# First norm from token-major sums and column halves of the conditioning; conditioning pieces closed one iteration later

## The chip, the cores and the metric

One NeuronCore of a Trainium2 chip runs the whole kernel. The metric is the device time of one execution in microseconds (us). Three runs of the kernel before gave 1294.48, 1294.83 and 1295.87 us, a median of 1294.83 us.

## The reference

One decoder layer for 512 tokens of width 1024, all in f32. A vector c of 1024 numbers is turned into nine vectors (shift, scale and gate for three sublayers), which steer the rest:

```python
mod = (silu(c) @ w_ada + b_ada).reshape(b_, 3, 3, d)           # w_ada: 1024 x 9216
h = modulate(rms_norm(x, norm_gains[0]), mod[:, 0, 0], mod[:, 0, 1])
x = x + 0.5 * mod[:, 0, 2] * swiglu(h, ffn1_w_in, ffn1_w_down) # 1024 -> 2 x 2816 -> 1024
h = modulate(rms_norm(x, norm_gains[1]), mod[:, 1, 0], mod[:, 1, 1])
...                                                            # projection, two gated recurrences, merge
x = x + mod[:, 1, 2] * (merged @ w_out)
h = modulate(rms_norm(x, norm_gains[2]), mod[:, 2, 0], mod[:, 2, 1])
x = x + 0.5 * mod[:, 2, 2] * swiglu(h, ffn2_w_in, ffn2_w_down)
return rms_norm(x, final_norm)
```

## The kernel before, in words

**Layout.** Activations lie channel-major: `X` is eight blocks of 128 channels by 512 tokens. Weights come in units of 1 MB (8 k-blocks by 256 columns) into `RAW`, two slots in turn. Each f32 value is split into a high and a low part: ScalarE writes the high part (`WH`, L873, `split_hi`), VectorE the rest (`WL`, L1200, `split_lo`), and TensorE takes three products per k-block and half of the columns (`three`, L478 to L480: WH by HH, WH by HL, WL by HH), 48 matmuls of 512 columns a unit. `HH` and `HL` are the same split of the normalised activation. Semaphores written by hand set the whole order: each engine has one list of instructions, and `unit_hi`, `unit_lo`, `unit_done`, `h_lo` count units and blocks.

**The conditioning.** The product silu(c) @ w_ada is made on VectorE: a piece is 512 columns of `w_ada`, and for each of the eight k-blocks `ada_term` (L1297, L1300) adds weight times one value per partition to `ACC`. A piece is closed on TensorE by eight one-column matmuls against ones, two for each 128 columns (`ada_reduce`, L608), and VectorE adds the bias into `MOD` (`add_ada_bias`, L1332). There are 18 pieces. The first four (shift and scale of the first sublayer) go through `ADA0`, 8 MB in eight transfers of two k-blocks; the other 14 through the two `ADAW` buffers, four transfers each (`load_ada`, L328), each of the last two waiting until VectorE is done with the buffer.

**The start.** x arrives token-major in `XST`. TensorE transposes it into channel blocks (L592), ScalarE copies each out of PSUM into `X` and squares it into `SG` (L882), GpSimd adds the squares into `S` (L423), TensorE sums over the partitions with a matmul against ones (L581), ScalarE makes the inverse root (`RMS`). Meanwhile VectorE works off the four pieces of `ADA0`, TensorE closes them (L599), VectorE makes scale and shift vectors (`vectors0`), splits the first unit, and then `normalise` and `norm_blocks` make block after block of `HH` and `HL`; the first unit's k-loop waits for each block.

**The loop of the first feed-forward part.** Eleven iterations of two units each (gate, up). In iteration i TensorE closes a piece of the conditioning before k-block 5 of the up unit; VectorE splits the next gate unit, adds that piece's bias (and so waits for the close), works off the next piece, multiplies gate by up (L1346), splits the next up unit. SyncE loads two units and a piece per iteration. After the loop the down projection closes two more pieces, and `first_units` of the mixing part the last one.

**The two later norms.** The last unit of a stage is done by token halves (`last_unit`), and `half_sum` (L551, L553, L556) sums squares of a half: three products, of `S` (blocks 0 to 5), of `SG` block 6 and of `SG` block 7, each as two matmul instructions.

## Time and profile before

| | |
|---|---|
| three runs, median | 1294.83 us |
| the profiled execution | 1293.82 us, of which its span is 1292.1 us |
| TensorE matmul busy | 1235.5 us (96%), 6099 matmuls |
| VectorE busy | 599.9 us (46%) |
| ScalarE busy | 415.4 us (32%) |
| GpSimd busy | 85.2 us (7%) |
| DMA | 143.40 MB, mean 111 GB/s |
| the three products of a k-block, activation side (L478 to L480) | 1064 times each, 383 to 392 ns a piece |

The busy share of TensorE is near the whole span, so what matters is where it does not run, or runs at the lower of its clock levels; VectorE and ScalarE are idle for half and more of the span. The span differs from the execution's time by 1.7 us, which lie before and after the first and last instruction.

### The profile page before, as it was taken

How to read it: one execution, taken by the hardware profiler on the slowest of the kernel's cores; microseconds unless marked ns; L12 is line 12 of the kernel's file. 1: busy time of each engine (PE TensorE's matmuls, PEld its weight loads, DVE VectorE, ACT ScalarE, POOL GpSimd, SP SyncE). 2: the span in 40 equal slices, each digit the busy share in tenths (PEclk: the TensorE clock that was granted, in tenths of full speed). 3: DMA queues.
4: the chain of work that ended last, by engine and by line, in shares of the span. 5: the costliest groups of instructions: out<-in, count | busy, mean ns of one | idle time of the engine just before them, and what ended most of it. 6: DMA issues, size and time to landing. Idle time of an engine off the chain costs nothing.

```text
span 1292.1 us, 15169 instructions
## 1 busy us (share of the span) xinstructions
PE 1235.5 (96%) x6099; PEld 1021.0 (79%) x6099; DVE 599.9 (46%) x714; ACT 415.4 (32%) x442; POOL 85.2 (7%) x121
## 2 busy tenths in 40 slices
PE   4699999999999999989999999999999999999996
PEld 3578888888889997867887788888988888888885
DVE  6855556456343667456645333335523233232221
ACT  4522322222222365343434322223422222222222
POOL 5100000000000032022310000000000000000000
PEclk9999999999999999988999999999999999999998
DMA  9276555555252422111221222243123332222311
GB/s 379 66 241 193 172 171 178 195 184 165 90 184 93 131 65 66 35 39 60 66 66 33 66 83 85 93 130 98 48 83 97 97 97 97 97 89 67 114 57 65
DMA packets 119789, 143.40 MB, mean 111 GB/s; under 512 B 3892, under 2 KB 102336, under 8 KB 119744
## 3 DMA queue, kind: packets, MB, share of 16 engines
q1 hardware_dynamic: 119560, 142.69, 33.6%
q8 instruction: 33, 0.54, 0.2%
q14 instruction: 12, 0.10, 0.0%
q10 hardware_dynamic: 184, 0.07, 0.0%
HBM read 140.65 MB, written 2.10 MB: 110 GB/s over the span
## 4 chain that ended last, share of the span: by engine, by line
issue 48%; PE 39%; DVE 6%; ACT 3%; DMA 2%; POOL 1%; SPq 0%; ACTq 0%; POOLq 0%; DVEq 0%
PE PS L478 10%; PE PS L480 10%; PE PS L479 10%; PE PS L682 3%; DVE ACC L1300 2%; PE PS L608 1%; ACT WH L873 1%; PE PS L521 1%; DMA RAW<-in_w_in_mix_dram 1%; PE PS L522 1%; PE PS L523 1%; DMA RAW<-in_ffn_w_in_dram 1%; DVE W L1440 1%; PE PS L722 1%; DVE WL L1200 0%
## 5 line engine op out<-in xcount | busy, mean ns | idle before, releaser
L478 PE MATMUL PS<-HH,WH 128*128 128x512 f32 (+1 forms) x1064 | 416.9, 392 | 7.4 <-DVE HL L1222 4.0
L479 PE MATMUL PS<-HL,WH 128*128 128x512 f32 (+1 forms) x1064 | 408.1, 384 | 0.0
L480 PE MATMUL PS<-HH,WL 128*128 128x512 f32 (+1 forms) x1064 | 408.0, 383 | 0.0
L1200 DVE TENSOR_TENSOR WL<-RAW,WH 128x2048 fp32r<-128x2048 f32 (+1 forms) x97 | 216.9, 2236 | 345.1 <-ACT WH L873 345.1
L873 ACT ACTIVATE WH<-RAW 128x2048 fp32r<-128x2048 f32 (+1 forms) x97 | 180.8, 1864 | 407.8 <-PE PS L480 370.6
L478 PEld LDWEIGHTS PS<-HH,WH 128*128 128x128 f32 x1064 | 201.2, 189 | 53.1 <-issue 6.8
L480 PEld LDWEIGHTS PS<-HH,WL 128*128 128x128 f32 x1064 | 201.1, 189 | 43.2
L479 PEld LDWEIGHTS PS<-HL,WH 128*128 128x128 f32 x1064 | 201.4, 189 | 41.3 <-issue 1.1
L478 PE MATMUL PS<-UH,WH 128*128 128x512 f32 (+1 forms) x372 | 140.2, 377 | 0.0
L479 PE MATMUL PS<-UL,WH 128*128 128x512 f32 (+1 forms) x372 | 139.8, 376 | 0.0
L480 PE MATMUL PS<-UH,WL 128*128 128x512 f32 (+1 forms) x372 | 139.6, 375 | 0.0
L1300 DVE SCALAR_TENSOR_TENSOR ACC<-ADAW,COND,ACC 128x512 f32<-128x512 f32 x98 | 73.7, 752 | 58.9 <-DMA ADAW<-in_w_ada_dram 56.2
L480 PEld LDWEIGHTS PS<-UH,WL 128*128 128x128 f32 x372 | 70.1, 188 | 13.7
L478 PEld LDWEIGHTS PS<-UH,WH 128*128 128x128 f32 x372 | 70.0, 188 | 13.6
L479 PEld LDWEIGHTS PS<-UL,WH 128*128 128x128 f32 x372 | 70.1, 188 | 13.5
L682 PEld LDWEIGHTS PS<-QP,KP 128*128 128x128 f32 (+1 forms) x384 | 50.8, 209 | 15.7 <-DVE KP L1455 10.5
L682 PE MATMUL PS<-QP,KP 128*128 128x64 f32 (+1 forms) x384 | 52.5, 294 | 8.8 <-DVE KP L1455 8.8
L980 ACT ACTIVATE SG<-PS 128x1024 f32<-128x1024 f32 x22 | 22.6, 1027 | 118.9 <-PE PS L480 116.7
L1346 DVE TENSOR_TENSOR SG<-SG,PS 128x1024 f32<-128x1024 f32 x22 | 26.8, 1218 | 60.2 <-PE PS L480 60.2
L1471 DVE COPY_PREDICATED SC<-MASK,PS 128x256 f32<-128x256 int8 x48 | 25.6, 533 | 42.3 <-PE PS L682 41.3
L882 ACT ACTIVATE SG<-X 128x512 f32<-128x512 f32 x28 | 17.7, 631 | 85.2 <-DVE X L1361 82.3
L984 ACT ACTIVATE UH<-SG 128x1024 f32 x22 | 23.2, 1053 | 63.7 <-DVE SG L1346 63.7
(225 smaller groups left out, 1187.6 us busy)
## 6 DMA issues: line engine op xcount, KB each, us to landing
RAW<-in_ffn_w_in_dram SPq DMA_DIRECT2D x44, 1024.0 KB, 5.2
ADAW<-in_w_ada_dram SPq DMA_DIRECT2D x56, 512.0 KB, 5.6
RAW<-in_w_in_mix_dram SPq DMA_DIRECT2D x22, 1024.0 KB, 5.2
RAW<-in_ffn_w_down_dram SPq DMA_DIRECT2D x16, 1024.0 KB, 5.2
ADA<-in_w_ada_dram SPq DMA_DIRECT2D x8, 1024.0 KB, 14.0
RAW<-in_ffn_w_down_dram SPq DMA_DIRECT2D x7, 768.0 KB, 4.8
RAW<-in_w_out_dram SPq DMA_DIRECT2D x3, 1024.0 KB, 5.1
XST<-in_x_dram SPq DMA_DIRECT2D x4, 512.0 KB, 5.1
```

Of the source, the lines that this page charges most:

```text
L478: mm(ps, whi, ahi, start=start, stop=False)
L479: mm(ps, whi, alo, start=False, stop=False)
L480: return mm(ps, wlo, ahi, start=False, stop=stop)
L682: ins = mm(PS[:, bank, 256 * j + 64 * t:256 * j + 64 * t + 64], KP[r, l, t * P:(t + 1) * P], QP[r, l, 64 * t:64 * t + 64], start=True, sto ...
L873: A(WH[slot(n)][:, 0:size], RAW[slot(n)][:, 0:size], ACT.Copy).then_inc(unit_hi, 1)
L882: A(SG[:, b % 2, :], ap, ACT.Square).then_inc(sq_ready, 1)
L980: A(SG[:, :, :], PS[:, 0:2, :], ACT.Silu).then_inc(silu_done, 1)
L984: A(UH[:, ds(2 * i, 2), :], SG[:, :, :], ACT.Copy).then_inc(u_hi, 1)
L1200: V.tensor_tensor(WL[s][:, 0:size], RAW[s][:, 0:size], WH[s][:, 0:size].bitcast(F32), ALU.subtract)\
L1300: V.scalar_tensor_tensor(acc_tile, w, COND[:, k:k + 1], acc_tile, ALU.mult, ALU.add).then_inc(ada_acc, 1)
L1346: V.tensor_tensor(SG[:, :, :], SG[:, :, :], PS[:, 2:4, :], ALU.mult).then_inc(umul_done, 1)
L1471: ins = V.copy_predicated(near, m, ps).then_inc(near_done, 1)
```

## The change

It rebuilds the start. The first four pieces of the conditioning are cut by columns into two halves: each half holds, for shift and for scale, the columns of four channel blocks, and is worked off with terms of 1024 columns instead of 512; k-block 1 of the first half goes to TensorE. `ADA0` comes in 16 transfers of one k-block, rows of 2 KB instead of 4 KB, and the first units' RAW comes in k-halves behind each half of `ADA0`. Sums of squares are made from token-major x on ScalarE (`accum_out`), one number per token, and the normalised blocks come from TensorE as x times a diagonal matrix of inverse roots (`normalised`), parked in `TN0`. The transposes that give `X` are spread between. The first two units run as k-blocks 0 to 3 of both, then 4 to 7 of both (`first_pair`). GpSimd no longer adds squares.

Each later piece is loaded and worked off one iteration later and closed in the gate unit of the iteration after; the last four are closed in the down projection (three) and in the output projection (one). At the two later norms the next unit's split is cut in two halves, the squares of block 6 are added to `S` on VectorE, and the sums take three products instead of six. The small inputs all go on ScalarE's queue; the two sigmoids of the lower bound move behind the loop.

```diff
-        ADA0 = place("ADA0", [P, 2, DB, 2 * AW], 0)
+        ADA0 = place("ADA0", [P, 2, DB, 2, AW], 0)
         XST = place("XST", [P, TT, D], 65536)
-        ACC0 = place("ACC0", [P, 4, AW], HO + 2 * H_BYTES - 4 * AW * 4)
+        ACC0 = [place("ACC0a", [P, 2 * AW], NT), place("ACC0b", [P, 2 * AW], 2 * FB * T * 4)]
+        TN0 = place("TN0", [P, DB, T], HO + H_BYTES)
+        DIAG = place("DIAG", [P, TT, P], 104448)
...
+        PE_TERMS = ((1,), ())
+        TN0_BANK = (4, 5, 7, 3, 4, 5, 7, 4)
+        TN0_AFTER = {4: 1, 5: 2, 6: 3, 7: 5}
...
+            def load_ada0(half):
+                for k in range(DB):
+                    sp.dma_start(ADA0[:, half, k, :, :], ada_parts[:, k, 0:2, AW * half:AW * (half + 1)])\
+                        .then_inc(ada0_in[DB * half + k], 16)
...
-            load(0, 0, raw(0), cols(w1, 0))
-            load(1, 1, raw(1), cols(w1, FF))
-            load_ada(4 * DB, slice(4 * AW, 5 * AW))
-
+            KH = DB // 2
+            load_ada0(0)
+            for n, col in ((0, 0), (1, FF)):
+                sp.dma_start(raw(n)[:, 0:KH, :], cols(w1, col, 0, KH)).then_inc(low_in[n], 16)
+            load_ada0(1)
+            for n, col in ((0, 0), (1, FF)):
+                sp.dma_start(raw(n)[:, KH:DB, :], cols(w1, col, KH, KH)).then_inc(raw_in[n], 16)
...
-                load_ada(5 * DB + DB * i, ds(AW * i + 5 * AW, AW))
+                load_ada(4 * DB + DB * i, ds(AW * i + 4 * AW, AW))
...
-                if j in (1, 5):
-                    piece = NP + 4 + (1, 5).index(j)
+                if j in (2, 5, 8):
+                    piece = NP + 3 + j // 3
...
+                if pair == 1:
                     piece = NP + 6
+                    sp.wait_ge(y_lo, 2 * HEADS)
                     load_ada(DB * piece, slice(piece * AW, (piece + 1) * AW))
...
-            nc.gpsimd.memset(S[:, :], 0.0).then_inc(sacc, 1)
-            for b in range(DB):
-                pool.wait_ge(sq_ready, b + 1)
-                pool.wait_ge(sacc, b + 1)
-                nc.gpsimd.tensor_tensor(S[:, :], S[:, :], SG[:, b % 2, :], ALU.add).then_inc(sacc, 1)
...
-                            if (th, m, k) == (1, 0, 4):
-                                at_mid()
+                            if (th, m, k) == sum_at:
+                                half_sum(e + 1, 0)
...
                 ps = PS[:, 7 - th, half_t(th)]
-                if blocks67 != 1:
-                    pe.wait_ge(sacc, 9 + 7 * g)
-                    if th and g == 1:
-                        pe.wait_ge(mod_ready, NP + 6)
+                if th == 0:
+                    pe.wait_ge(sacc, SACC_LAST[g] + 8)
                     mm(ps, ONES[:, :], S[:, half_t(th)], start=True, stop=False)
-                    pe.wait_ge(sq_ready, 8 + 10 * (g - 1) + 7 + 2 * th)
-                    mm(ps, ONES[:, :], SG[:, 0, half_t(th)], start=False, stop=False)
-                if blocks67 != 0:
-                    pe.wait_ge(sq_ready, 8 + 10 * (g - 1) + 8 + 2 * th)
+                    pe.wait_ge(sq_ready, 8 + 10 * (g - 1) + 8)
                     mm(ps, ONES[:, :], SG[:, 1, half_t(th)], start=False, stop=True).then_inc(ssq_done, 1)
-
-            def first_units(n0, banks, g, between=None):
+                else:
+                    pe.wait_ge(sacc, SACC_LAST[g] + 10)
+                    pe.wait_ge(mod_ready, NP + 5 + g)
+                    mm(ps, ONES[:, :], S[:, half_t(th)], start=True, stop=True).then_inc(ssq_done, 1)
...
+            def normalised(b):
+                if b in TN0_AFTER:
+                    pe.wait_ge(tn_copied, TN0_AFTER[b])
+                for t in range(TT):
+                    ins = mm(PS[:, TN0_BANK[b], t * P:(t + 1) * P], XST[:, t, b * P:(b + 1) * P], DIAG[:, t, :],
+                             start=True, stop=True)
+                ins.then_inc(tn_done, 1)
...
+            def ada0_reduce(half):
+                pe.wait_ge(ada_acc, 16 * half + 16)
+                for s, m, col in ada0_columns(half):
+                    whole = not PE_TERMS[half]
+                    ins = mm(PS[:, 6, col:col + 1], ACC0[half][:, AW * s + m * P:AW * s + (m + 1) * P],
+                             ONES[:, 0:1], start=whole, stop=whole or (s, m) == (1, 3))
+                ins.then_inc(ada_red, 2)
+            for b in (0, 1, 2):
+                transpose_x(b)
+            pe.wait_ge(cond_ready, 1)
+            for k in PE_TERMS[0]:
+                pe.wait_ge(ada0_in[k], 16)
+                for j, (s, m, col) in enumerate(ada0_columns(0)):
+                    mm(PS[:, 6, col:col + 1], ADA0[:, 0, k, s, m * P:(m + 1) * P], COND[:, k:k + 1],
+                       start=k == PE_TERMS[0][0] and j == 0, stop=False)
+            pe.wait_ge(small_ready, 1)
+            pe.wait_ge(dg_ready, TT)
+            for b in range(4):
+                normalised(b)
+            pe.wait_ge(xready, 3)
+            transpose_x(3)
+            ada0_reduce(0)
+            for b in (4, 5):
+                normalised(b)
...
+            def first_pair():
+                for n in range(2):
+                    pe.wait_ge(low_lo, n + 1)
+                    whi, wlo = weights(n)
+                    for k in range(DB // 2):
+                        if n == 0 and k == 3:
+                            normalised(6)
+                        if n == 1 and k == 1:
+                            normalised(7)
+                        if n == 1 and k == 2:
+                            for b in (4, 5, 6):
+                                pe.wait_ge(tn_copied, b + 2)
+                                transpose_x(b)
+                        if n == 1 and k == 3:
+                            pe.wait_ge(mod_ready, 2)
+                            ada0_reduce(1)
+                        pe.wait_ge(h_lo, k + 1)
+                        for m in range(2):
+                            w = slice(m * P, (m + 1) * P)
+                            three(PS[:, 2 * n + m, :], whi[:, k, w], wlo[:, k, w], HH[:, k, :], HL[:, k, :], k == 0, False)
...
-                             before=ada_reduce_at(5, 5 * DB + DB * i, 4 + i) if with_ada and half == 1 else None)
+                             before=ada_reduce_at(5, 4 * DB + DB * i, 3 + i) if with_ada and half == 0 else None)
...
+                ins = A(TN0[:, 2 * t:2 * t + 2, :], XST[:, t, :], ACT.Square, accum_out=SS[:, t:t + 1])
+            ins.then_inc(ss_done, 1)
+            act.wait_ge(consts, 7)
+            act.wait_ge(ss_done, 1)
+            A(R4[:, :], SS[:, :], ACT.Ln, bias=EPST[:, 0:1], scale=1.0 / D).then_inc(first_ln, 1)
+            act.wait_ge(first_ln, 1)
+            A(R4[:, :], R4[:, :], ACT.Exp, scale=-0.5).then_inc(first_r, 1)
+            act.wait_ge(first_r, 1)
+            for t in range(TT):
+                A(DIAG[:, t, :], IDENT[:, :], ACT.Copy, scale=R4[:, t:t + 1]).then_inc(dg_ready, 1)
...
+            low_half(0)
+            act.wait_ge(av_half, 1)
+            first_block(0)
+            first_block(1)
+            low_half(1)
+            first_block(2)
+            first_block(3)
+            for b in range(4, DB):
+                park(b)
+            for b in range(4, 7):
+                copy_x(b, b + 1)
+            for n in range(2):
+                act.wait_ge(raw_in[n], 16)
+                A(WH[n][:, half_unit:UNIT], RAW[n][:, half_unit:UNIT], ACT.Copy).then_inc(unit_hi, 1)
+            act.wait_ge(av_ready, 1)
+            for b in range(4, DB):
+                first_block(b)
+            copy_x(7, 8)
...
+            def next_hi(n, part):
+                if part == 0:
+                    act.wait_ge(raw_in[slot(n)], raw_value(n))
+                    act.wait_ge(unit_done, n - 1)
+                half = UNIT // 2
+                cut = slice(part * half, (part + 1) * half)
+                A(WH[slot(n)][:, cut], RAW[slot(n)][:, cut], ACT.Copy).then_inc(unit_hi if part else next_half, 1)
+            def last_blocks(g, x0, sacc0, n):
+                if g == 1:
+                    next_hi(n, 0)
+                    next_hi(n, 1)
...
-                half_block(g, 0, 2)
-                half_block(g, 0, 3)
+                for b in range(2, 6):
+                    half_block(g, 0, b)
                 half_rms(g, 1)
-                for b in range(4, DB):
...
+            for k in range(DB):
+                if k not in PE_TERMS[0]:
+                    ada0_term(0, k)
+            low_split(0)
+            vectors0(0)
+            dve.wait_ge(tn_copied, 1)
+            first_lo(0)
+            first_lo(1)
+            low_split(1)
+            first_lo(2)
+            ada0_term(1, 0)
+            first_lo(3)
+            for k in range(1, DB):
+                ada0_term(1, k)
+            high_split(0)
+            vectors0(1)
+            first_lo(4)
+            first_lo(5)
+            high_split(1)
+            first_lo(6)
+            first_lo(7)
...
```

(`low_split` and `high_split` are `split_lo` on half a unit, `park` copies a normalised block from PSUM to `TN0`, `first_block` makes `HFULL` and `HH` of a block, `first_lo` its `HL`, `ada0_term` is a term of 1024 columns, `vectors0(half)` the bias and scale of one half.)

TensorE's list from its first instruction (PST: small inputs; XST: x; ACC: sums of conditioning terms; HH, WH: activation and weight, high parts). Before:

```order
L586 MATMUL PS<-IDENT,PST 128x124
L592 MATMUL PS<-IDENT,XST 128x128 x32
L581 MATMUL PS<-S,ONES 128x512
L599 MATMUL PS<-ONES,ACC_72 128x1 x16
...
L478 MATMUL PS<-HH,WH 128x512
```

And in the change:

```order
L598 MATMUL PS<-IDENT,PST 128x124
L603 MATMUL PS<-IDENT,XST 128x128 x12
L633 MATMUL PS<-COND,ADA_70 128x1 x8
L611 MATMUL PS<-DIAG,XST 128x128 x16
L603 MATMUL PS<-IDENT,XST 128x128 x4
L623 MATMUL PS<-ONES,ACC0a 128x1 x8
L611 MATMUL PS<-DIAG,XST 128x128 x8
L494 MATMUL PS<-HH,WH 128x512
```

Sixteen of the 32 transposes, the sum of squares and half of the closing matmuls no longer stand ahead of the first product; eight one-column products of the conditioning and 24 products with the diagonal now do.

VectorE's list from the end of the start into the loop (ADAW: the later pieces; SG: gate times up). Before, where the first of the later pieces stood ahead of the loop:

```order
L1222 TENSOR_TENSOR HL<-HFULL,HH 128x512 x2
L1297 TENSOR_SCALAR ACC<-ADAW_65,COND 128x512
L1300 SCALAR_TENSOR_TENSOR ACC<-ADAW_65,COND,ACC 128x512
...
L1200 TENSOR_TENSOR WL<-RAW,WH 128x2048
...
L1332 TENSOR_TENSOR MOD<-PS,PT 128x4
```

And in the change, where this is iteration 0, written out ahead of the loop:

```order
L1496 TENSOR_TENSOR HL<-HFULL,HH 128x512 x2
L1344 TENSOR_TENSOR WL<-RAW,WH 128x2048
L1461 TENSOR_SCALAR ACC<-ADAW_65,COND 128x512
L1464 SCALAR_TENSOR_TENSOR ACC<-ADAW_65,COND,ACC 128x512
...
L1556 TENSOR_TENSOR SG<-SG,PS 128x1024
L1344 TENSOR_TENSOR WL<-RAW,WH 128x2048
```

The piece has moved behind the split of the next gate unit.

## Rows read from the trace of the kernel before

**Rows 1.** The page: TensorE's share of the span

```profile
PE 1235.5 (96%) x6099; PEld 1021.0 (79%) x6099; DVE 599.9 (46%) x714; ACT 415.4 (32%) x442; POOL 85.2 (7%) x121
```

**Rows 2.** Timeline of TensorE, 8 to 48 us: start, length, work, [idle before <- releaser]

```profile
9.22 3.62 PE L592 MATMUL PS<-IDENT,XST 128*128 128x128 f32 x16
...
27.48 2.08 PE L581 MATMUL PS<-S,ONES 128*128 128x512 f32 x2 [9.35 <-POOL S L423]
29.35 3.57 PE L599 MATMUL PS<-ONES,ACC 128*128 128x1 f32 x16
39.52 3.58 PE L599 MATMUL PS<-ONES,ACC 128*128 128x1 f32 x16 [6.59 <-DVE ACC L1300]
47.11 0.77 PE L478 MATMUL PS<-HH,WH 128*128 128x512 f32 x1 [4.01 <-DVE HL L1222]
```

**Rows 3.** The chain that ended last, 9 to 48 us: start, length, work

```profile
13.83 4.17 DVE ACC L1300 x4
...
34.65 2.12 DVE ACC L1300 x4
...
46.27 0.69 DVE HL L1222
```

**Rows 4.** DMA in 40 slices of 1 us, 0 to 40 us

```profile
GB/s 0 36 202 381 401 419 408 428 415 430 414 418 430 414 430 414 422 422 418 430 414 430 414 422 422 414 434 379 388 379 347 351 349 199 0 0 0 0 0 33
```

**Rows 5.** Timeline of ScalarE, 9 to 44 us

```profile
10.01 1.28 ACT L962 ACT_TABLE_LOAD   x1
...
12.92 0.60 ACT L967 ACTIVATE X<-PS 128x512 f32<-128x512 f32 x1
...
43.61 0.81 ACT L944 ACTIVATE HH<-TN,MOD,AV 128x512 fp32r<-128x512 f32 x1 [7.29 <-DVE AV L1282]
```

**Rows 6.** The page: groups of instructions, xcount | busy, mean ns | idle before

```profile
L1200 DVE TENSOR_TENSOR WL<-RAW,WH 128x2048 fp32r<-128x2048 f32 (+1 forms) x97 | 216.9, 2236 | 345.1 <-ACT WH L873 345.1
L873 ACT ACTIVATE WH<-RAW 128x2048 fp32r<-128x2048 f32 (+1 forms) x97 | 180.8, 1864 | 407.8 <-PE PS L480 370.6
...
L984 ACT ACTIVATE UH<-SG 128x1024 f32 x22 | 23.2, 1053 | 63.7 <-DVE SG L1346 63.7
```

**Rows 7.** Timeline of TensorE, 51 to 53 us

```profile
51.51 0.63 PE L479 MATMUL PS<-HL,WH 128*128 128x512 f32 x1
...
51.94 0.44 PE L480 MATMUL PS<-HH,WL 128*128 128x512 f32 x1
...
52.44 0.40 PE L479 MATMUL PS<-HL,WH 128*128 128x512 f32 x1
```

**Rows 8.** The chain that ended last, 60 to 125 us

```profile
95.11 0.79 PE PS L608 x8
...
118.31 0.79 PE PS L608 x8
```

**Rows 9.** Timeline of VectorE in one iteration of the loop, 96 to 110 us

```profile
96.17 0.16 DVE L1332 TENSOR_TENSOR MOD<-PS,PT 128x4 f32 x1 [2.03 <-PE PS L608]
96.32 0.49 DVE L1297 TENSOR_SCALAR ACC<-ADAW,COND 128x512 f32<-128x512 f32 x1
...
105.91 1.22 DVE L1346 TENSOR_TENSOR SG<-SG,PS 128x1024 f32<-128x1024 f32 x1
```

**Rows 10.** Timeline of TensorE at the second norm, 436 to 438 us

```profile
436.78 0.59 PE L551 MATMUL PS<-S,ONES 128*128 128x256 f32 x2
...
437.21 0.59 PE L553 MATMUL PS<-SG,ONES 128*128 128x256 f32 x2
```

**Rows 11.** Waits of TensorE, 0 to 1292 us: who for whom, us, times, longest

```profile
PE PS L682 <- DVE KP L1455: 8.8, 3, 3.2
...
PE PS L553 <- ACT SG L901: 2.0, 2, 1.1
PE PS L478 <- DVE HL L1250: 1.0, 2, 0.5
```

**Rows 12.** Stretch 513 to 520 us: PE busy, PEclk, DMA share, GB/s

```profile
513.00:520.00 7.00, 6.97 (x25) 0.52 0.05 7
```

342 lines of the change are left out of this document (214 added, 128 removed).

## The prediction, made before the run

> **What bounds the kernel now.** I read the page first. TensorE is busy for 96% of the span [rows 1], so time can only be had where it waits, where it runs at the lower of its two clock levels, or where it does work that can go. Then I read its timeline over the first 48 us [rows 2]. The first product of the first unit starts at 47.11 us. Before it stand 16 transposes in 3.62 us, 9.35 us of waiting for GpSimd's sums, a first close of conditioning pieces (3.57 us), 6.59 us of waiting for VectorE's terms, a second close of 3.58 us, and 4.01 us for the first block of HL. The reader is to see that this stretch is a chain and no throughput limit of TensorE. The chain of waits says whose it is [rows 3]: terms of the conditioning on VectorE. Four of them take 4.17 us while GpSimd adds squares and 2.12 us later, when it only builds masks. The transfers are no longer the last to arrive: at about 420 GB/s they are through at 34 us [rows 4].
>
> In the loop TensorE is the bound. From one close to the same point of the next iteration is 118.31 - 95.11 = 23.20 us [rows 8], of which 0.79 is the close and 22.41 the 96 products of 0.233 us. From the close at 95.11 to the end of iteration 1 are 0.79 + 18 x 0.233 = 5.0 us, so that iteration ends at 100.1, and the loop nine iterations of 23.20 later, at **308.9 us**. I measure the change by that point.
>
> **The change: the way to the first product.** TensorE starts at 9.2 us as before. Twelve transposes at 3.62/16 = 0.226 us take it to 11.9. The eight one-column products of the conditioning cost what a close of that size costs: in the rows sixteen instructions, two to a product, last 3.57 us [rows 2], so 15.5. It then needs the diagonal.
>
> ScalarE comes from the table load at 10.01 + 1.28 = 11.3 us [rows 5]. Four squares of 1024 columns have no row; a 1024-column pass takes 1.05 us on average [rows 6], and I take 4 x 1.05 = 4.2 us, to 15.5. Bounds: 4 x 0.9, if the passes overlap, to 4 x 1.35, if writing the sum costs 0.3 each. Logarithm, exponential and four small copies I put at 1.5 us: **17.0 us** for the diagonal.
>
> Then 16 diagonal products, 32 instructions of 128 columns. At the transposes' pace that is 7.2 us; at double the clock 3.6. The main products ran 0.43 us apart until 51.94 and 0.25 afterwards (two in 0.50) [rows 7], that is at 1.2 GHz and then 2.4, although the granted clock of that stretch reads full; the change came 4.8 us after dense work began. The transposes of 9.2 to 12.8 did not bring it. I take a rise part of the way: the sixteen end at 23.1 (bounds 20.6 and 24.2).
>
> The Trainium skill, "TensorE: Matmul & The Clock Gate", section "What's actually happening", has the default state throttled and activity releasing it. By that rule alone, with the seven microseconds of earlier small products counted as activity, the sixteen would run at the full level throughout and the sum come out 2.5 us lower; the transposes' row speaks against so early a rise, the later rows agree with a rise.
>
> Behind the sixteenth product two paths lead to the first scale vectors. TensorE: four transposes and the close of the first half, 0.5 + 1.6 us at the upper level, 0.9 + 3.6 at the lower. ScalarE and VectorE: park a block (0.6), copy a block of X (0.6 after its transposes), split half a unit (1.86/2 = 1.0, then 2.24/2 = 1.2 on VectorE, which stands ahead of the vectors in its list) [rows 5, 6]: 3.6 to 3.9 us. So the vectors start at **27.0 us** (bounds 24.4 and 28.8). VectorE's own seven wide terms are not last: rows 3 give 0.53 us for 512 columns when two sums alternate and rows 9 0.8 when one sum waits for itself, so a wide term is 0.8 + 0.5 = 1.3; with the transfers at 420 GB/s (6.3 MB, about 19 us [rows 4]) they end at 20.3. With 0.4 us for the vectors, 0.8 for HH [rows 5] and 0.7 for HL [rows 3] the first product starts at **29 us** instead of 47.11.
>
> **From there to the end of iteration 0.** Now VectorE is last. From 28.9 on: HL 1 at 30.4, half a split to 31.9, HL 2 to 32.9, a term to 33.8, HL 3 to 34.5, seven wide terms of 1.3 to 43.7 (bounds 1.06 and 1.5 a term, 42.0 and 45.1). TensorE has its 48 products and the diagonal ones done by then or nearly, closes the second half until 45.3, vectors 45.7, HH 46.5, HL 47.2: k-blocks 4 to 7 begin. ScalarE needs two passes of 0.75 us a block, TensorE 6 x 0.233 = 1.4, with half a split between: the gate unit ends at 53.6, the up unit 24 products later, at **59.3 us**.
>
> **Iteration 1.** Its close now stands in the gate unit, at k-block 5, and needs the piece that VectorE does in iteration 0. From 53.6: gate function 1.03, split 1.9 on ScalarE and 2.3 on VectorE, to 58.8; the piece takes from 96.32 to 105.9 [rows 9], 9.6 us with its waits for ADAW, to 68.4. TensorE is there at 59.3 + 30 x 0.233 = 66.3: a new wait of **2.1 us**. In every later iteration the split is done 17.3 us after the iteration's start, the piece at 26.9, and it is needed at 30.2: 3.3 us in hand, no wait. Nor for gate times up: it comes 3.7 us late, now 5.8, but is needed 12 us in. So iteration 1 ends at 59.3 + 23.2 + 2.1 = 84.6, the loop at 84.6 + 208.8 = 293.4: **15.5 us** earlier.
>
> **Behind the loop.** TensorE has the same 14 closes, but four behind the loop in place of three: +0.8. In the down projection a piece of 9.6 us stands in front of splits that have 2.8 to 3.6 us to spare by the same count; SyncE's next load is queued behind the piece's third and fourth transfer and lands some 24 us into a pair whose split it must precede at 26. In the output of the mixing part the same, with 5 us to spare. I cost these at nothing; without that cover each costs up to 3 us. The two sums lose three products each, 0.43 us apiece [rows 10], and their waits of 2.0 and 1.0 us in all [rows 11] largely go: 2.6 + 3.0 = 5.6 at most. But at the second norm the sum stands only one quarter (18 products of 256 columns, about 2.1 us) ahead of the next unit, and its way through ScalarE and VectorE takes 2.9, and after it the two engines that make the blocks set the pace of the first unit. I take 2.1 us for both norms together (bounds 0 and 5). The small moved operations (sigmoids with two table loads, 2.6 us on ScalarE) lie in the 11 us in which its next split waits for TensorE.
>
> **The sum:** 15.5 - 0.8 + 2.1 = 16.8 us. Against the profiled execution's 1293.8 that is 1277.0; the median of the three runs stands 1.0 above it, hence **1278**. Its own range: 2.5 us less and 1.8 more for the clock at the start, 1.5 either way for the wide terms, 2 either way at the norms, 1.4 for the squares: 1273 to 1284. A measurement of this kernel tells 0.2%, 2.6 us, from no change.
>
> **Rivals.**
> A faster end: the diagonal products run at the upper level, the squares overlap, and both norms give all they can: 2.5 + 0.6 + 1.5 + 2.9 off: 1271. For it: every bound is one a row allows. Against: all must fall one way. 0.12.
>
> The clock falls elsewhere. In the mixing part TensorE runs at about half clock for 513 to 520 us [rows 12], behind one of three waits for VectorE of about 3 us [rows 11], and about 3.4 us are lost each time. The stage arrives 17 us earlier, with one conditioning piece less beside it and one more later; a fourth such fall, plus the lower level to the first product, gives 1278 + 3.4 + 1.8 + 1.5 = 1285. Against: three runs within 1.4 us say that where falls come is stable. 0.10.
>
> The start does not shorten as written: the instruction stream of TensorE's now unrolled start, or the 2 KB rows, hold it while the DMA engines are full, or the transfers of the second half bound the way to k-block 4. If the loop starts only 5 us earlier than before, 1289 to 1291. Against: the total of the bytes is the same and was in at 34 us, well ahead of 43.7. 0.05.
>
> **The other side**, slower: the close in the gate unit waits in every iteration. Its place is L608's wait on ACC; its price w, nine times. It decides the sign from 9w > 16.8 + 2.6, w = 2.2, that is if a piece takes 9.6 + 3.3 + 2.2 = 15.1 us; at 15.5 us the time is 1278 + 23 = 1301. For it: the loop already keeps VectorE 5.8 us behind TensorE when gate times up starts. Against: the longest piece so far is near 10 us. 0.03.
>
> Forecast 0.70. Faster by over 0.2%: forecast, the first two rivals and most of the third, 0.95; within it 0.02; slower 0.03. The range of 1271 to 1287 leaves out part of the third rival and the fourth, and a little at the low end.
>
> **What would show it.** First main product at 29 us (26 to 32); the diagonal at 17; GpSimd without adds; closes of 1-column products at 21 to 28 and at 44; iteration 0 over at 59; one wait of TensorE on ACC of about 2 us in iteration 1 and none after; closes 23.20 apart; no wait on SG at the norms, but one on HL at the second norm. The prediction is wrong if the first product starts after 35, if the loop's period grows, or if the splits of the down projection become last.

## The result, and the profile after

The changed kernel takes **1287.67 us** (median of 6 runs, 1283.97 to 1290.56), the kernel before, run beside it, 1294.65 us (1292.57 to 1296.10). The ratio is 0.9946 with a 95% interval of 0.9928 to 0.9964: faster, by 7.0 us or 0.5%, where 16.8 were forecast. The profiled execution took 1287.32 us, its span is 1285.6 us. That is 10.3 us more than the 1277.0 that the prediction's sum gave for a profiled execution.

TensorE's timeline of the changed kernel over its first 46 us (start, length, work, and the idle time before it with what ended it) answers to [rows 2]:

```profile
9.49 2.77 PE L603 MATMUL PS<-IDENT,XST 128*128 128x128 f32 x12
12.18 3.54 PE L633 MATMUL PS<-COND,ADA 128*128 128x1 f32 x16
17.93 5.28 PE L611 MATMUL PS<-DIAG,XST 128*128 128x128 f32 x32 [2.21 <-ACT DIAG L1066]
23.05 0.60 PE L603 MATMUL PS<-IDENT,XST 128*128 128x128 f32 x4
23.48 1.84 PE L623 MATMUL PS<-ONES,ACC0a 128*128 128x1 f32 x16
25.19 2.03 PE L611 MATMUL PS<-DIAG,XST 128*128 128x128 f32 x16
28.60 0.47 PE L494 MATMUL PS<-HH,WH 128*128 128x512 f32 x1 [1.38 <-DVE HL L1496]
...
43.42 2.19 PE L623 MATMUL PS<-ONES,ACC0b 128*128 128x1 f32 x16 [0.86 <-DVE ACC0b L1475]
45.47 0.78 PE L494 MATMUL PS<-HH,WH 128*128 128x512 f32 x1
46.05 0.63 PE L495 MATMUL PS<-HL,WH 128*128 128x512 f32 x1
```

In place of the waits of 9.35, 6.59 and 4.01 us stand waits of 2.21 and 1.38, and the first main product starts at 28.60 us instead of 47.11: the start did what it was forecast to do. The last two rows show something else: behind the second close, products start 0.43 us apart, so TensorE runs at its lower level for 3.4 us.

The waits of TensorE over the whole changed kernel (who for whom, us in all, times, longest), against [rows 11]:

```profile
PE PS L762 <- DVE KP L1666: 8.6, 3, 3.1
PE PS L494 <- DVE HL L1390: 4.1, 7, 1.2
PE PS L650 <- DVE ACC L1464: 2.3, 1, 2.3
```

The wait for SG at the two later norms is gone, and that for HL has grown from 1.0 to 4.1 us. The wait on ACC occurs once, as forecast.

TensorE's timeline at the closes of iterations 1, 2 and 3:

```profile
69.48 1.05 PE L650 MATMUL PS<-ONES,ACC 128*128 128x1 f32 x8 [2.32 <-DVE ACC L1464]
...
92.95 0.95 PE L650 MATMUL PS<-ONES,ACC 128*128 128x1 f32 x8
...
116.32 0.84 PE L650 MATMUL PS<-ONES,ACC 128*128 128x1 f32 x7
```

No later close waits, yet two of them stand 116.32 - 92.95 = **23.37 us** apart, where [rows 8] had 23.20 (23.19 in most iterations). The iteration has the same 96 products and one close, and TensorE never idles in it. Each product has become 1.8 ns longer, and 3708 of that size read HH, HL, UH or UL in the kernel. The prediction had named it as one of three signs of being wrong: "if the loop's period grows". Nothing in the diff above speaks of it, and the experiments began here. The point by which the prediction measures the change, the first product behind the loop, comes at 296.29 us (forecast 293.4, before 308.8):

```profile
296.29 0.40 PE L494 MATMUL PS<-UH,WH 128*128 128x512 f32 x1
```

In the numbers below, the **pace** is the mean distance between the starts of neighbouring 512-column products, taken over five long stretches without waits. It is 0.2323 us in the kernel before and 0.2342 in the changed one. Once, in the second feed-forward part of the first profile of the kernel before, it was 0.2333, and not in a second execution of it.

### The profile page after: what moved, and what is told of

It is laid out like the page before. It is cut to its first block, busy times and chain, and to the rows that moved or that the text cites. A ratio compares the mean times of both kernels' runs of the same rounds, so it can differ in the third digit from the quotient of the medians.

```text
span 1285.6 us, 15227 instructions
## 1 busy us (share of the span) xinstructions
PE 1244.0 (97%) x6165; PEld 1027.7 (80%) x6165; DVE 586.0 (46%) x702; ACT 418.8 (33%) x457; POOL 69.9 (5%) x112
## 4 chain that ended last, share of the span: by engine, by line
issue 48%; PE 42%; DVE 5%; ACT 3%; DMA 1%; POOL 1%; ACTq 0%; POOLq 0%; DVEq 0%; SPq 0%
PE PS L494 11%; PE PS L496 11%; PE PS L495 11%; PE PS L762 3%; PE PS L650 1%; DVE ACC0b L1475 1%; PE PS L537 1%; PE PS L538 1%; PE PS L539 1%; ACT WH L950 1%; DVE W L1651 1%; PE PS L802 1%; DMA PST<-in_lb_logits_dram 0%; PE PS L611 0%; PE PS L789 0%
## 5 line engine op out<-in xcount | busy, mean ns | idle before, releaser
L1344 DVE TENSOR_TENSOR WL<-RAW,WH 128x2048 fp32r<-128x2048 f32 (+2 forms) x93 | 207.7, 2233 | 361.7 <-ACT WH L950 361.7
L950 ACT ACTIVATE WH<-RAW 128x2048 fp32r<-128x2048 f32 (+2 forms) x93 | 173.2, 1862 | 391.4 <-PE PS L496 336.1
L537 PE MATMUL PS<-WH,HH 128*128 128x256 f32 x128 | 37.8, 295 | 0.0
L959 ACT ACTIVATE SG<-X 128x512 f32<-128x512 f32 x20 | 12.6, 632 | 75.9 <-DVE X L1574 75.8
```

Source lines behind the costliest of these rows:

```text
L537: mm(ps, HH[:, k, tok], whi[:, k, :], start=k == 0, stop=False)
L950: A(WH[slot(n)][:, 0:size], RAW[slot(n)][:, 0:size], ACT.Copy).then_inc(unit_hi, 1)
L1344: V.tensor_tensor(WL[s][:, 0:size], RAW[s][:, 0:size], WH[s][:, 0:size].bitcast(F32), ALU.subtract)\
```

## The experiments

### 1. The 16 bytes

The change adds one small tile, `SS`, 16 bytes per partition, ahead of the large arena that holds HH, HL, UH, UL and most else. It takes 32 bytes, so all activation tiles move by 32 bytes against X, RAW, WH and WL, which lie ahead of it. Four kernels: both kernels again, the change with `SS` laid over another small tile (so nothing moves), and the kernel before with an unused tile of the same size.

```diff
-        SS = sb("SS", [P, TT])       # in the change: after_ss_in_v4
+        SS = V4
...
+        SS = sb("SS", [P, TT])       # in the kernel before: before_pad
```

> The kernel before once more, for a profile on the same chip as the three beside it. In the two profiles so far the 512-column products of the feed-forward loops start 0.2323 us apart in the kernel before and 0.2342 us in the changed one (0.8% more), which over the span is about 7 of the 10 us by which the prediction missed. Theory A (the pace comes with the chip or the moment, not with the kernel): this run shows the same pace as the changed kernel beside it. Theory B (the new 16-byte tile SS moves the arena with HH, HL, UH, UL by 32 bytes, and the pace of the products hangs on where their moving operand starts): 0.2323 here. Theory C (something else in the changed kernel slows the products): 0.2323 here too.

> The changed kernel once more. A: its pace of products equals that of the kernel before beside it, and the time is about 1277 to 1281 us if the kernel before gives 1294. B and C: 0.2342 us a product and 1284 to 1290 us, as before.

> The changed kernel with the sums of squares kept in the tile V4, which is free until the end, so that no tile is added and the arena starts where it did in the kernel before. B: 0.2323 us a product in the loop, 6 to 8 us faster than the changed kernel, 1278 to 1281 us. A and C: no difference from the changed kernel beyond 1 us.

> The kernel before with one unused 16-byte tile added at the place of SS, nothing else. B: 0.2342 us a product and 6 to 8 us slower than the kernel before, 1300 to 1303 us. A and C: the time of the kernel before within 1 us.

Measured, beside a kernel before of 1292.4 us: same_before 1290.3 in one run; same_after 1287.99 (12 runs, ratio 0.9972, 0.9956 to 0.9989); after_ss_in_v4 **1281.94** (0.9927, 0.9910 to 0.9945); before_pad **1297.3** (1.0048, 1.0030 to 1.0067). Pace 0.2323, 0.2342, 0.2323, 0.2342. The changed kernel, measured again, gains only 0.3% where it gained 0.5% at first: its single executions spread from 1283.0 to 1293.5 us, more than those of the others.

So an unused tile alone makes the kernel before slower, by 4.9 us (the expectation asked for 6 to 8; the interval holds 4 to 9), and the change without the shift is 6 us faster than with it, against 3708 x 0.0019 = 7.0 us by the pace. The closes of after_ss_in_v4 are 23.19 apart again, but its iteration 1 has a stretch that the changed kernel's has not. Its timeline of TensorE:

```profile
69.47 1.82 PE L650 MATMUL PS<-ONES,ACC 128*128 128x1 f32 x8 [1.84 <-DVE ACC L1464]
71.16 0.77 PE L494 MATMUL PS<-HH,WH 128*128 128x512 f32 x1
71.73 0.63 PE L495 MATMUL PS<-HL,WH 128*128 128x512 f32 x1
...
76.00 0.57 PE L496 MATMUL PS<-HH,WL 128*128 128x512 f32 x1
76.40 0.39 PE L494 MATMUL PS<-HH,WH 128*128 128x512 f32 x1
```

From the close to 76.2, products are 0.43 us apart: 6.8 us at the lower level, some 3.4 us lost, behind a wait shorter than the 2.32 us that left the clock alone in the changed kernel. Without that fall its 1281.9 would be 1278.5, by this estimate.

### 2. The wait of iteration 1, the terms, the adds, and 64 bytes

Three edits each ask for one term of the prediction. v4_close_in_up moves the later pieces' close from the gate unit to k-block 1 of the up unit, 24 products or 5.6 us later (its expectation says 3.6, which is a slip), so that TensorE need not wait in iteration 1. v4_narrow_terms works the second half's seven terms as 14 of 512 columns on two alternating sums. before_no_adds takes GpSimd's adds out of the kernel before: it then writes the constant 8.0 instead of the sum of squares of the first norm. before_pad64 shifts the tiles of the kernel before by 64 bytes.

```diff
-                             before=ada_reduce_at(5, 4 * DB + DB * i, 3 + i) if with_ada and half == 0 else None)
+                             before=ada_reduce_at(1, 4 * DB + DB * i, 3 + i) if with_ada and half == 1 else None)
...
-                    V.scalar_tensor_tensor(ACC0[half][:, :], w, COND[:, k:k + 1], ACC0[half][:, :], ALU.mult, ALU.add)\
-                        .then_inc(ada_acc, 2)
+                for s in range(2):
+                    acc, ws = ACC0[half][:, AW * s:AW * (s + 1)], w[:, AW * s:AW * (s + 1)]
...
+                        V.scalar_tensor_tensor(acc, ws, COND[:, k:k + 1], acc, ALU.mult, ALU.add).then_inc(ada_acc, 1)
...
-                nc.gpsimd.tensor_tensor(S[:, :], S[:, :], SG[:, b % 2, :], ALU.add).then_inc(sacc, 1)
+                nc.gpsimd.memset(S[:, :], 8.0).then_inc(sacc, 1)
...
+        PAD = sb("PAD", [P, 16])
```

> after_ss_in_v4 with the close of the loop's pieces moved from k-block 5 of the gate unit to k-block 1 of the up unit, 3.6 us later in each iteration. Theory D (the close in the gate unit of iteration 1 is the new wait, 2.2 us, and the fall of the clock at 69.5 us in the profile of after_ss_in_v4, 6.8 us at half rate, comes with it): no wait on ACC above 0.5 us in iteration 1, no fall of the clock near 70 us, and 2 to 5 us faster than after_ss_in_v4, 1277 to 1280 us. Theory E (the wait only hides another one, the split or the gate multiplication of iteration 1, and the fall has another cause): the same time within 1 us.

> after_ss_in_v4 with each term of 1024 columns done as two of 512 that take turns. Theory F (a chained wide term costs more, 1.40 us in the profile, than two alternating ones, 1.06 to 1.27 us, and VectorE is last on the way to k-block 4): seven terms of the second half take 7.4 to 8.9 us instead of 9.8, the second half closes 1 to 2 us earlier and the time is 1 to 2 us lower. Theory G (fewer instructions are better, as the drain behind each VectorE instruction costs): the seven take 10.4 us or more and the time is 1 us higher.

> The kernel before with GpSimd's eight adds of squares replaced by memsets of the sum to a constant of the usual size (the first norm's root is then that of a constant, all else as before). It prices one part of the change alone, that GpSimd no longer adds beside VectorE. Theory H (the shared path of GpSimd and VectorE slowed the terms, 4.17 to 5.16 us for four instead of 2.12): the second close starts at 34 to 36 us instead of 39.5 and the first product of the first unit at 41 to 43 instead of 47.1. Theory I (the transfers pace the terms there, and the adds only fill their waits): the close stays within 1 us of 39.5.

> The kernel before with an unused tile of 64 bytes, so that the arena starts 64 bytes later (89920, a multiple of 64 but not of 128) where before_pad had it 32 bytes later (89888). Theory B1 (the products slow down when their activation operand starts off a multiple of 64 bytes): 0.2323 us a product and the time of the kernel before within 2 us. Theory B2 (it takes a multiple of 128 or more, or any move of the arena against the weight slots costs): 0.2342 us and 5 to 7 us slower.

**v4_close_in_up: 1278.2 us** (1276.84 to 1279.11; beside 1291.02; ratio 0.9901, 0.9885 to 0.9916). Its row at the place of the old wait:

```profile
71.75 0.50 PE L494 MATMUL PS<-HH,WH 128*128 128x512 f32 x1 [0.91 <-DVE WL L1344]
```

It no longer waits on ACC, but 0.91 us on WL, and no product near 70 us runs at the lower level: theory D held, with 3.7 us gained over after_ss_in_v4. The loop ends at 292.68 us, 15.2 us before the second trace of the kernel before (307.89). That this equals the forecast's 15.5 is half a coincidence, as the wait of 2.1 us in the forecast is gone here and 1.7 us at the lower level at 45 us were not in it. The time is the forecast's 1278, at the old place of the tiles.

**v4_narrow_terms: 1281.3 us** (1279.93 to 1283.21, ratio 0.9927), as without it. VectorE's rows for the seven wide terms in the changed kernel and for the fourteen narrow ones here:

```profile
33.49 9.79 DVE L1475 SCALAR_TENSOR_TENSOR ACC0b<-ADA,COND,ACC0b 128x1024 f32<-128x1024 f32 x7
```

```profile
33.66 9.36 DVE L1477 SCALAR_TENSOR_TENSOR ACC0b<-ADA,COND,ACC0b 128x512 f32<-128x512 f32 x14
```

A wide term is 1.40 us, two narrow ones 1.34. Counted from the first product, the second close begins 0.4 us earlier than in after_ss_in_v4 (14.4 us against 14.8), and the time does not show it. Neither of its two theories held.

**before_no_adds: 1285.42 us** in one run, 5.6 less than the kernel before beside it. VectorE's row for 14 terms of the first two pieces, in the kernel before and then here, and TensorE's of the second close here:

```profile
12.51 17.45 DVE L1300 SCALAR_TENSOR_TENSOR ACC<-ADA,COND,ACC 128x512 f32<-128x512 f32 x14
```

```profile
12.99 9.36 DVE L1300 SCALAR_TENSOR_TENSOR ACC<-ADA,COND,ACC 128x512 f32<-128x512 f32 x14
```

```profile
31.81 3.58 PE L599 MATMUL PS<-ONES,ACC 128*128 128x1 f32 x16 [2.87 <-DVE ACC L1300]
```

The fourteen take 9.36 us instead of 17.45, the second close comes at 31.81 instead of 39.52, and the first product at 39.40 instead of 47.11. So taking the adds out is worth 7.7 of the 18.5 us by which the changed kernel starts its products earlier, though GpSimd still writes into S here. Term by term, in the kernel before eight of them start 1.67 us apart while GpSimd adds, and 0.66 apart once it builds masks; here all start 0.66 apart, beside GpSimd's constants as beside its masks. That VectorE is slowed by GpSimd is what the Trainium skill describes in "SBUF — State Buffer", section "Who interferes with whom": one pair of ports shared by the two under an exclusive lock, for which a VectorE instruction with two inputs in SBUF contends with a GpSimd instruction that reads SBUF. The rows agree, with 1.67 us a term while GpSimd reads and adds and 0.66 when it only writes.

The same traces correct a reading of the prediction. The pieces of [rows 3] leave out what the chain lists between them as "issue", 1.54 us behind the 4.17 and 0.53 behind the 2.12. Four terms beside the masks therefore take 2.65 us from start to start, not 2.12, and a term is 0.66 and not 0.53.

**before_pad64: 1293.4 us** (10 runs, ratio 1.0020, 1.0010 to 1.0029), pace 0.2333: between the places of 0 and 32 bytes. No rule of one step fits, so the place itself had to be mapped.

### 3. Which tiles, which distance

```diff
+        PAD = sb("PAD", [P, 24])     # after SS: all activation tiles +128 (after_shift128)
...
-        HO = ARENA                   # in the kernel before: HH, HL alone +32 (before_h32)
+        HO = ARENA + 32
...
-            last_unit(0, UH, UL, 16, False, (1, 1, 0))     # sums_earlier
-            last_unit(1, MH, ML, 0, True, (1, 0, 6))
+            last_unit(0, UH, UL, 16, False, (1, 0, 3))
+            last_unit(1, MH, ML, 0, True, (1, 0, 3))
```

> The change with 96 bytes more behind SS, so that the activation tiles lie 128 bytes behind their place in the kernel before instead of 32. Theory (the pace of a 512-column product hangs on the place of the activation tiles within a line of 128 bytes or of less): pace 0.2323 us instead of 0.2342, and the time falls from 1288 to 1282, that of SS over V4, ratio 0.993. Rival (any other place than the old one is slower, or the shift of 96 bytes more makes it slower again, as an absolute place would): pace 0.234 or more, time 1288 or more. A pace between, as with 64 bytes (0.2333), would say that the step of 128 is not the whole period: 1285.

> The kernel before with only HH and HL (and what lies over them at the ends of stages) 32 bytes further on; UH, UL and all weight tiles stay. Theory (it is the operand that streams through TensorE whose place counts): pace 0.2342 us where HH and HL are the operands (the pair units of both feed-forward parts and the projection), 0.2323 in both down projections; time 1291.5 + about 0.9% of the 60% that run on HH, some 5 to 6 us: 1297. Rival (the distance between activation and weight tiles, or the place of something else in the shifted arena): 0.2323 everywhere and 1291.5; or 0.2342 everywhere.

> The close-in-up kernel with the first half of the two later norms' sums taken three k-blocks (nine products of 256 columns, 1.1 us) earlier in the last unit. Theory (after each norm TensorE waits for the first block of HL, 0.5 and 1.2 us, because the way from the sum through ScalarE and VectorE is longer than what is left of the unit): the first of these waits goes at both norms, and up to 1.1 us per norm is gained, time 1278.2 less 1 to 2: 1276.5. Rival (the squares of blocks 6 and 7 are late, so TensorE now waits at the sum for S or SG instead, as L553 did before): a wait of 0.5 to 1.1 us on S or SG appears, the time stays 1278 or rises. A second rival: ScalarE and VectorE set the pace of all blocks, so the second wait of 1.2 us grows by what the first loses: 1278.

> The change with SS laid over V4 (activation tiles at their old place), with the later pieces closed before k-block 1 of the up unit (as the close-in-up run) and with the seven terms of the second half as two alternating terms of 512 columns (as the narrow-terms run), all at once. Theory: the first two are worth what they gave alone, the third gives 0.4 us of VectorE and nothing of the time, so 1278 us (1275 to 1280) beside a before of 1291 to 1292, ratio 0.990; second close at 43.0, no half clock near 70, closes 23.19 apart. Rival: with the second close earlier and the one in iteration 1 gone, iteration 0 ends 0.4 us earlier and another 0.4 us falls out of the time: 1277.6. Not to be told from the theory by time, only by the start of the second close and of the down projection (292.3 against 292.7).

**after_shift128: 1264.83 us** (1263.48 to 1265.91, beside 1293.45; ratio 0.9775, 0.9759 to 0.9792). The expectation was wrong by 17 us, to the good side. The pace is neither that of the old place nor slower, but 0.2268 us. Two closes of its timeline are 22.71 us apart:

```profile
119.36 0.95 PE L651 MATMUL PS<-ONES,ACC 128*128 128x1 f32 x8
...
142.07 0.94 PE L651 MATMUL PS<-ONES,ACC 128*128 128x1 f32 x8
```

**before_h32: 1298.63 us** (1297.50 to 1300.32, ratio 1.0041, 1.0025 to 1.0057). The pace is 0.2340 to 0.2343 in the pair units, which run on HH and HL, and 0.2323 in both down projections, which run on UH and UL. Its closes (the loop runs on HH):

```profile
96.73 0.95 PE L608 MATMUL PS<-ONES,ACC 128*128 128x1 f32 x8
...
120.10 0.95 PE L608 MATMUL PS<-ONES,ACC 128*128 128x1 f32 x8
```

The time is 5.2 us above the kernel before, as expected. So it is the tiles that TensorE reads as products' operands whose place counts, not that of anything else in the arena.

**sums_earlier: 1278.26 us** (ratio 0.9888, 0.9871 to 0.9906), as v4_close_in_up. At the second norm the first wait on HL is gone and the way from the last unit to the next stage is 9.62 us instead of 10.18; the second wait stays. TensorE's rows for the second norm, of v4_close_in_up and of sums_earlier:

```profile
420.44 0.36 PE L494 MATMUL PS<-HH,WH 128*128 128x256 f32 x1 [0.54 <-DVE HL L1390]
...
422.66 0.39 PE L494 MATMUL PS<-HH,WH 128*128 128x256 f32 x1 [0.16 <-DVE HL L1390]
...
427.92 0.39 PE L494 MATMUL PS<-HH,WH 128*128 128x256 f32 x1 [1.22 <-DVE HL L1390]
```

```profile
423.43 0.39 PE L494 MATMUL PS<-HH,WH 128*128 128x256 f32 x1 [0.16 <-DVE HL L1390]
...
428.70 0.39 PE L494 MATMUL PS<-HH,WH 128*128 128x256 f32 x1 [1.22 <-DVE HL L1390]
```

Of the 0.56 us, 0.34 are given back before the stage's third unit, and at the third norm nothing is gained at all (12.37 us both). The sums are not what sets these stretches.

**best_combined: 1281.3 us** (1279.87 to 1284.96, ratio 0.9903, 0.9889 to 0.9918), the ratio of v4_close_in_up, though the expectation had the time at 1278. In its trace, which is that of the slowest of its five runs, the lower level at 46 us lasts 6.8 us (3.4 there), TensorE then waits 2.21 us on WL at 75.36 and its clock falls again for 6.8 us, so that the down projection begins at 299.5 us instead of the expected 292.3 to 292.7. Whether the edit on VectorE moved the fall or this one execution happened to have it is not shown.

### 4. Distance or place

The last five runs had to say whether the place of the streamed tiles counts or their distance from the weights, what other distances give, and whether this is apart from the change.

```diff
+        PAD = sb("PAD", [P, 32])     # ahead of the arena: tiles +128 (close_in_up_128, before_128)
...
+        PAD = sb("PAD", [P, 32])     # ahead of WH: WH, WL and tiles +128 (weights_too_128)
...
+        PAD = sb("PAD", [P, 48])     # tiles +192, and below HH, HL +224 (places_192_224)
...
-        HO = ARENA
+        HO = ARENA + 32
...
+        PAD = sb("PAD", [P, 24])     # tiles +96, and below HH, HL +160 (places_96_160)
...
-        HO = ARENA
+        HO = ARENA + 64
```

> The close-in-up kernel with the activation tiles 128 bytes further on. Theory (pace and order of the work are independent): pace 0.2268 us, and what the shift gave the change (1281.9 to 1264.8, 17 us) comes off 1278.2: 1261 us beside a before of 1291 to 1293, ratio 0.976. Rival (with quicker products TensorE waits longer for VectorE in iteration 1, or the clock falls there again): a wait on WL or ACC near 70 of 1.5 us or more with half clock behind it, and 1264 or 1265, no better than the change with the shift alone.

> The close-in-up kernel with 128 bytes inserted ahead of WH: the split weights WH and WL and the activation tiles all lie 128 bytes further on, so that their distance is that of the kernel before. Theory D (the distance between the streamed operand and the weight tile that is being loaded beside it counts): pace 0.2323 us again, 1278 us. Theory A (the place of the streamed operand alone counts): pace 0.2268 us, 1261 us. Some third pace would say that the weights' place counts by itself as well.

> The close-in-up kernel with UH and UL 192 bytes further on than in the kernel before, HH and HL 224. Theory P (a period of 128 bytes in the loss that 32 and 64 bring, and 128 a step of its own): paces of 0.2278 (192) and 0.2287 (224, by the 32's 0.0019) or so, time 1263. Rival M (the pace depends on how near the place is to 128 off the weights, falling to both sides): 192 like 64, 0.233; 224 like 32, 0.2342; time 1286. In the profile the down projections show 192, the up units 224.

> The close-in-up kernel with UH and UL 96 bytes further on, HH and HL 160. Theory P (128 is a step of its own, 32 more costs 0.0019 us there too): 96 near 0.2325 to 0.234, 160 near 0.2287; time 1266. Rival M (falls to both sides of 128 alike): 96 and 160 the same, some 0.230; time 1271.

> The kernel before with the activation tiles 128 bytes further on. Theory (the pace is apart from the change): pace 0.2268 us, and what the shift gave the change and the close-in-up kernel (17 and 18 us) comes off here too: 1291.5 less 17 is 1274, ratio 0.986; against it the change at the same places (1264.8) then stands 9 us lower, as it does at the old place (1291 against 1282). Rival (the kernel before has more of its time in waits and gains less): 1277 or more.

| kernel | us (range, runs) | ratio (95%) | pace, us |
|---|---|---|---|
| close_in_up_128 | 1259.61 (1258.25 to 1261.10, 5) | 0.9752 (0.9735 to 0.9769) | 0.2267 to 0.2272 |
| weights_too_128 | 1277.09 (1276.23 to 1278.12, 4) | 0.9892 (0.9874 to 0.9911) | 0.2323 to 0.2324 |
| places_192_224 | 1276.93 (1273.83 to 1280.66, 4) | 0.9892 (0.9866 to 0.9918) | 0.2290 in the down units, 0.2333 in the pair units |
| places_96_160 | 1279.99 (1279.37 to 1281.21, 4) | 0.9915 (0.9897 to 0.9933) | 0.2333 in both |
| before_128 | 1272.84 (1270.31 to 1274.06, 4) | 0.9857 (0.9840 to 0.9873) | 0.2267 to 0.2272 |

weights_too_128 decides the first question. It has its activation tiles where close_in_up_128 has them and only its weights (with the small tiles between the two) elsewhere; with the distance back at its old value, pace and time are back too. Closes of weights_too_128, and then of close_in_up_128:

```profile
97.11 0.95 PE L651 MATMUL PS<-ONES,ACC 128*128 128x1 f32 x8
...
120.30 0.95 PE L651 MATMUL PS<-ONES,ACC 128*128 128x1 f32 x8
```

```profile
98.54 0.95 PE L651 MATMUL PS<-ONES,ACC 128*128 128x1 f32 x8
...
121.25 0.95 PE L651 MATMUL PS<-ONES,ACC 128*128 128x1 f32 x8
```

By distance (in bytes, against the kernel before): 0 gives 0.2323, 32 gives 0.2342, 64, 96, 160 and 224 give 0.2333, 192 gives 0.2290 and 128 gives 0.2268. Neither of the two expectations on other places held: not a period of 128 bytes, and not a fall to both sides of 128 alike (96 and 160 are alike, 64 and 192 are not). Whether 256 bytes is a period was not tried.

before_128 shows that the pace adds to the change and takes nothing of it: the kernel before gains 19 us by it (0.9857), and the change some 20 against its form at the old place (0.9927 to 0.9775). With the same places in both, the change is then worth 8 us by the medians (1272.84 to 1264.83) and 11 by the ratios, against 9 at the old place. In close_in_up_128 TensorE waits 1.2 us on WL near 74 us, with no fall of the clock behind it; the rival of its expectation asked for 1.5 us or more and a fall. **close_in_up_128, at 1259.61 us, is 2.5% below the kernel before** and the fastest of all.

## Why the prediction was wrong

**Right: the way to the first product.** Forecast 29, measured 28.60 us. ScalarE's rows of the changed kernel for the four squares and the diagonal:

```profile
11.58 1.06 ACT L1057 ACTIVATE TN<-XST 128x1024 f32<-128x1024 f32 x1
12.54 0.19 ACT L1057 ACTIVATION_READ_ACCUMULATOR TN<-XST 128x1 f32 x1
12.63 1.04 ACT L1057 ACTIVATE TN<-XST 128x1024 f32<-128x1024 f32 x1
...
16.51 1.28 ACT L1066 ACTIVATE DIAG<-IDENT,R 128x128 f32<-128x128 f32 x4
```

A square costs 1.05 us from start to start, as I took it; writing the sum is an instruction of its own of 0.19 us, most of which overlaps. The diagonal was done at 17.8, forecast 17.0, and the 16 diagonal products took 5.1 us from 17.93 on, forecast 6.1. They ended at 23.1 as forecast because the two errors cancel, which is luck. Their instructions start 0.21 us apart until 21.04 us and 0.11 apart from there on, so the rise part of the way did happen.

**Nearly right: iteration 0.** The second close was to begin at 43.7 and began at 43.42. Here too two errors cancel: a wide term is 1.40 us and not 1.3 (the 0.53 read off [rows 3] is 0.66 from start to start, as before_no_adds showed), and the seven terms began 1.0 us earlier than forecast, at 33.49. HL of block 4 was to be ready at 47.2 and was at 47.72, and TensorE, busy without a gap since 45.47 and at its lower level until 48.2, came to k-block 4 at 48.18. So the gate unit ends about 54.6 instead of 53.6, and the iteration at 59.9 instead of 59.3.

**Right in kind: iteration 1.** The wait is 2.32 us (forecast 2.1), but the close comes at 69.48 (forecast 68.4). The piece takes 9.5 us, from 59.73, where 9.6 were forecast with its waits; what is late is its start (forecast 58.8), by what the gate unit of iteration 0 ended late. VectorE's rows for six of its seven sums, with the waits for the third and fourth transfer:

```profile
61.50 1.54 DVE L1464 SCALAR_TENSOR_TENSOR ACC<-ADAW,COND,ACC 128x512 f32<-128x512 f32 x2 [0.51 <-DVE ACC L1464]
65.50 1.54 DVE L1464 SCALAR_TENSOR_TENSOR ACC<-ADAW,COND,ACC 128x512 f32<-128x512 f32 x2 [2.46 <-DMA ADAW<-in_w_ada_dram]
67.80 1.54 DVE L1464 SCALAR_TENSOR_TENSOR ACC<-ADAW,COND,ACC 128x512 f32<-128x512 f32 x2 [0.76 <-DMA ADAW<-in_w_ada_dram]
```

**Wrong: "so iteration 1 ends ..., the loop at 84.6 + 208.8", nine iterations of 23.20.** This is the step that failed, and it failed again, unwritten, in all that follows: the prediction carried the length of a product over from the kernel before as if the change could not touch it. Each iteration is 0.18 us longer, and the cause is the shift of the activation tiles by 32 bytes against the weights, as before_pad and after_ss_in_v4 show from both sides. The 2652 products of this size behind the loop make 2652 x 0.0019 = 5.0 us, less 1.0 because the first profile of the kernel before had its second feed-forward part at 0.2333.

**Wrong too: "I take 2.1 us for both norms together".** The worth is about none. In the change at the old place (after_ss_in_v4), against the second trace of the kernel before (same_before), the way to the third stage's first product is 2.41 us shorter (14.78 to 12.37) and the stage behind it 2.13 us longer (247.78 to 249.91); at the second norm 0.39 shorter and 0.79 longer, the latter with a close of 0.9 less in it. That is a loss of 1.0 us; against the first trace, whose way at the second norm is 11.80 us instead of 10.58, it is a gain of about 0.3. The wait for SG went, and 3.1 us more of waiting for HL came: the blocks through ScalarE and VectorE set the pace, the reason that the prediction gave for its bounds. It should have taken the lower of them, or less. The closes behind the loop were right: 0.9 each for one more.

**A term not in the sum: the clock's falls.** The changed kernel has the lower level at 44.9 us for 3.4 us, behind the close of one-column products, and in the mixing part for 27.3 us against 23.9 in the kernel before. In its first profile the last of the four falls of that part begins at 635.4 us and lasts 10.2, in the second it begins at 707.0 and lasts 3.4, and the second profiles of both kernels have 20.5 us each. So this difference is one between executions, and no run shows that the change brought it. The rows are those of 635 to 645 us, first of the first profile (PE busy with its count, then columns as in [rows 12] but for all engines), then of same_after:

```profile
635.00:645.00 10.00, 10.00 (x31) 7.32 (x32) 2.43 (x3) 3.95 (x5) 0.00 (x0) 0.52 0.00 0
```

```profile
635.00:645.00 10.00, 10.00 (x49) 7.38 (x48) 3.15 (x3) 3.96 (x5) 0.00 (x0) 1.00 0.07 16
```

TensorE is busy without a gap in both, with 31 instructions in one and 49 in the other, and granted clocks of 0.52 and 1.00.

**The sum of it,** from the forecast's 1277.0 to the 1287.3 of the profile: the loop 2.9 (1.6 of pace, 1.1 of the late close of iteration 1), the pace behind it 4.0, more time at the lower level 1.7, and the norms, with what is left over, about 1.7. That is 10.3. Of these 5.6 us are the pace; without it the time would be 1282, inside the range. The rivals: "the clock falls elsewhere" had a part in it, 1.7 of the 7 us that it named; the start and the close of every iteration, the other two that ended high, did not happen.

## What to carry to other kernels

A diff that adds a small tile moves every tile that is allocated behind it. Where TensorE is the bound, compare the distance between two like points of the steady loop in both traces before explaining anything else: 0.18 us in 23.2 named the cause here, and trying eight distances between activation and weight tiles was worth more (19 us) than the whole change (9 us at the old place). A wait that TensorE can be spared is worth more than its length where it stands ahead of a fall of the clock (3.7 us for moving a close that waited 1.84), and work that is taken ahead of a norm gives nothing when the blocks behind it are what is late.

## What the runs showed of the hardware

**The length of a 512-column product depends on where its two operands lie against each other.** From 0.2268 to 0.2342 us, 3.3%, by 128 or 32 bytes, within 0.0005 the same in all stretches of a kernel and in all kernels with the same distance, but for the stretch named at the end. Only one run moves the weights, so that the distance alone decides rests on that one. The Trainium skill, "SBUF — State Buffer", section "SBUF: two separate sides", says that within the engine side only the port pair shared by GpSimd and VectorE causes contention. By that rule all eight distances should have given one pace; weights_too_128 against close_in_up_128, 0.2323 against 0.2268, speaks against it, at least for what TensorE itself reads. That its loading of the next weights (0.19 us beside each product in the profile) meets its reading of the streamed operand is my reading of it; no run takes the one away and leaves the other. What else could carry it, such as ScalarE and VectorE writing the same tiles, is not excluded, though the down units of before_h32 kept their pace while the pair units of it lost theirs.

**The length of a wait does not settle whether the clock falls behind it.** At the close of iteration 1, waits of 2.32 and 1.88 us left the clock up in the two traces of the changed kernel; 1.84 us in after_ss_in_v4, 1.93 in v4_narrow_terms and 2.69 in after_shift128, with the same instructions behind, came ahead of a fall of 6.8 us. The fall of 3.4 us before it began at 44.9 and 44.8 us in the first two and at 45.6, 45.2 and 47.0 in the others. Why is open; it wasn't tried.

**In one stretch the pace is not a constant of the kernel.** In the second feed-forward part, traces at distance 0 show 0.2324 in some executions (same_before, v4_close_in_up, weights_too_128) and 0.2333 in others (the first of the kernel before, best_combined, sums_earlier). That is 1 us, and its cause is open. A step of 0.001 us in a single stretch therefore proves no shift; at 64 bytes it stands in all four stretches of before_pad64.
